# Gathering an expert's tokens: 32 one-hot products or an indirect DMA and 8 transposes

## What is computed

```python
def swiglu(h, w_gate, w_up, w_down):
    return (jax.nn.silu(h @ w_gate) * (h @ w_up)) @ w_down

def moe_ffn(h, w_router, w_gate, w_up, w_down):
    ...
    logits = (hf @ w_router).astype(jnp.float32)
    top_vals, top_idx = lax.top_k(logits, TOP_K)
    top_w = jax.nn.softmax(top_vals, axis=-1)
    gates = jnp.einsum('nk,nke->ne', top_w, jax.nn.one_hot(top_idx, N_EXPERTS, dtype=jnp.float32))
    out = jnp.zeros_like(hf)
    for e in range(N_EXPERTS):
        out = out + gates[:, e:e + 1].astype(hf.dtype) * swiglu(hf, w_gate[e], w_up[e], w_down[e])
```

## Time and profile before

| what | us |
|---|---|
| median of three runs | 1322.89 (1321.39 to 1323.42) |
| the profiled execution, its own time | 1321.78 |
| its span in the profile | 1320.0 |
| from the first gather's start to the last gather's last part | 504.5 to 1302.7 |

### The profile page before, as it was taken

One profiled execution on the slowest core, in us unless ns is written; L12 is line 12 of the kernel. 1 busy time (PEld: TensorE's weight loads), 2 busy tenths in 40 slices (PEclk: granted clock), 3 DMA queues, 4 the chain that ended last, 5 costly groups with the idle time before them and its releaser, 6 DMA issues.

```text
span 1320.0 us, 18637 instructions
## 1 busy us (share of the span) xinstructions
PE 1260.0 (95%) x6834; PEld 1070.5 (81%) x6834; DVE 1011.0 (77%) x1083; ACT 828.8 (63%) x877; POOL 117.7 (9%) x121
## 2 busy tenths in 40 slices
PE   6898899999899888999999999999999999999997
PEld 6776799999787676888888888888888888888885
DVE  5886654455579747888888888888888887887985
ACT  5356444433544745777777777777777777777774
POOL 2860000000069001000000000000000000000000
PEclk9899999999899797999999999999999999999998
DMA  9400665555442039999999999999999999999950
GB/s 327 147 20 1 206 215 190 182 179 184 123 156 76 17 120 361 377 361 327 356 366 328 351 364 332 347 367 329 348 365 329 350 364 329 348 363 332 349 216 32
DMA packets 174725, 344.40 MB, mean 261 GB/s; under 512 B 5558, under 2 KB 63476, under 8 KB 174676
## 3 DMA queue, kind: packets, MB, share of 16 engines
q1 hardware_dynamic: 173852, 341.27, 73.4%
q0 software_dynamic: 624, 1.93, 0.4%
q10 hardware_dynamic: 200, 0.54, 0.1%
HBM read 342.67 MB, written 1.05 MB: 260 GB/s over the span
## 4 chain that ended last, share of the span: by engine, by line
PE 87%; DVE 7%; ACT 3%; issue 2%; DMA 0%; SPq 0%; POOL 0%; POOLq 0%; DVEq 0%; ACTq 0%
PE bank L1432 26%; PE bank L1434 26%; PE bank L1433 26%; PE bank L1714 3%; PE bank L1734 1%; DVE cv L1086 1%; PE bank L1529 1%; DVE lo_ring L965 1%; DVE xn L1086 1%; ACT hi_ring L658 1%; PE bank L1569 1%; PE bank L1726 1%; PE bank L1727 1%; PE bank L1511 0%; DMA vec_rows<-in_diff_subln 0%
## 5 line engine op out<-in xcount | busy, mean ns | idle before, releaser
L970 DVE TENSOR_TENSOR lo_ring<-raw_m,hi_ring 128x2048 fp32r<-128x2048 f32 x168 | 382.6, 2288 | 51.2 <-ACT hi_ring L664 51.1
L664 ACT ACTIVATE hi_ring<-raw_m 128x2048 fp32r<-128x2048 f32 x168 | 322.2, 1919 | 84.6 <-PE bank L1434 84.6
L1432 PE MATMUL bank<-hi_ring,hT_hi 128*128 128x512 f32 (+2 forms) x896 | 336.3, 375 | 0.0
L1434 PE MATMUL bank<-hi_ring,hT_lo 128*128 128x512 f32 (+2 forms) x896 | 329.6, 368 | 0.0
L1433 PE MATMUL bank<-lo_ring,hT_hi 128*128 128x512 f32 (+2 forms) x896 | 329.0, 367 | 0.0
L970 DVE TENSOR_TENSOR lo_ring<-raw_a,hi_ring 128x2048 fp32r<-128x2048 f32 x96 | 219.3, 2291 | 41.0 <-ACT hi_ring L664 41.0
L664 ACT ACTIVATE hi_ring<-raw_a 128x2048 fp32r<-128x2048 f32 x96 | 183.4, 1918 | 57.5 <-PE bank L1434 57.5
L965 DVE TENSOR_TENSOR lo_ring<-raw_a,hi_ring 128x2048 fp32r<-128x2048 f32 (+2 forms) x59 | 131.8, 2236 | 96.3 <-ACT hi_ring L658 96.3
L1432 PEld LDWEIGHTS bank<-hi_ring,hT_hi 128*128 128x128 f32 x896 | 169.6, 189 | 30.6 <-DVE lo_ring L970 2.4
L1434 PEld LDWEIGHTS bank<-hi_ring,hT_lo 128*128 128x128 f32 x896 | 169.4, 189 | 28.7
L1433 PEld LDWEIGHTS bank<-lo_ring,hT_hi 128*128 128x128 f32 x896 | 169.7, 189 | 27.4 <-issue 0.5
(11 more groups left out here) (266 smaller groups left out, 1421.9 us busy)
## 6 DMA issues: line engine op xcount, KB each, us to landing
raw_m<-in_w_down_exp SPq DMA_DIRECT2D x80, 1024.0 KB, 5.4
raw_a<-in_w_up_exp SPq DMA_DIRECT2D x48, 1024.0 KB, 5.7
raw_m<-in_w_gate_exp SPq DMA_DIRECT2D x48, 1024.0 KB, 5.6
raw_a<-in_w_gate_exp SPq DMA_DIRECT2D x40, 1024.0 KB, 5.7
raw_m<-in_w_up_exp SPq DMA_DIRECT2D x40, 1024.0 KB, 5.9
raw_a<-in_w_in SPq DMA_DIRECT2D x12, 1024.0 KB, 7.0
raw_a<-in_w_gate_dense SPq DMA_DIRECT2D x11, 1024.0 KB, 5.4
raw_a<-in_w_up_dense SPq DMA_DIRECT2D x11, 1024.0 KB, 5.5
```

The lines of the kernel that those rows point to most:

```text
L664: A(hi_of(NA + j), t, ACT.Copy).then_inc(hi_ready, 1)
L970: V.tensor_tensor(lo_of(NA + j), expert_slot(i, j)[0], hi_of(NA + j).bitcast(F32), ALU.subtract).then_inc(lo_ready, 1)
L1432: M(o, lh, rh, start=start, stop=False)
L1434: return M(o, ll, rh, start=False, stop=stop)
```

## The change

- A new DRAM tensor `rows_dram` holds the normed rows with their gain, float32. POOL writes it from `xn` with two DMAs of 512 KB after line 627, ahead of its load of `g_bc`. ACT waits for both before its first step of item 0, since `m_sg` overwrites `xn`.
- Item 0 is gathered as before. For each later item PE makes two products of `onehot` with a column of token numbers, `tok_r`, after the first part of G4 of the item ahead; they give the token number of each slot. DVE casts it to an integer, `slot_i`, at the first part of U4. POOL then issues one indirect DMA: 128 rows of 4 KB from `rows_dram` into `xg`, which is the second half of `xn`.
- In the place of the 32 products stand 8 transposes of `xg`, into banks 6 and 7. ACT copies their high part into `sel_hi`, two instructions in the place of four; DVE subtracts it from the banks into `sel_lo`, two new instructions, ahead of `y_lo`. G0 of the next item now waits for DVE there.
- DVE no longer waits for the earlier gather before it makes a new `onehot`. ACT copies `tok_r` once in the setup, and the table of constants is 4 columns wider.

```diff
+            for t in range(TT):
+                pool.dma_start(rows_dram[t * P:(t + 1) * P, :], xn[:, t, :]).then_inc(rows_out, 16)
             pool.dma_start(g_bc[:], a["final_norm"].rearrange("(o d) -> o d", o=1).broadcast_to([P, D])
                            ).then_inc(gfin_in, 16)
+
+            def fetch(i, first=False):
+                if not first:
+                    pool.wait_ge(pad_done, i)
+                pool.wait_ge(slot_ready, i + 1)
+                nc.gpsimd.tensor_tensor(pool_pad[:], half_neg[:], half_neg[:], ALU.mult).then_inc(pad_done, 1)
+                nc.gpsimd.indirect_dma_start(xg, None, rows_dram, bass.IndirectOffsetOnAxis(slot_i[:, 0:1], 0),
+                                             bounds_check=T - 1, oob_is_err=False
+                                             ).then_inc(xg_in, 16)
+
+            pool.wait_ge(rows_out, 16 * TT)
+            fetch(0, first=True)
...
+            with pool.Fori(1, n_items) as i:
+                fetch(i)
             norm_pow(2 * LAYERS)
...
+            def fetched_evac(i):
+                for h in range(2):
+                    act.wait_ge(gather_mm, 4 + 2 * i + h + 1)
+                    A(sel_hi[:, 4 * h:4 * h + 4, :], bank[6 + h][:].rearrange("p (k s) -> p k s", k=4),
+                      ACT.Copy).then_inc(gathered, 1)
...
-                gather_evac(i + 1)
+                fetched_evac(i)
                 act.wait_ge(piece_used, expert_done(i, "D", EC - 1))
...
-            gather_evac(0)
+            first_gather_evac()
+            act.wait_ge(rows_out, 16 * TT)
             item(0, True)
...
-                        dve.wait_ge(gather_mm, 4 + 4 * i)
                         dve.wait_ge(onehot_done, 3 + 3 * i)
                         make_onehot(i + 1)
                         dve.wait_ge(route_v, rv[0] + 1 + i)
+                    if kind == "U" and c == 4 and part == 0:
+                        dve.wait_ge(slot_mm, i + 1)
+                        V.tensor_copy(slot_i[:], bank[7][:, 0:1]).then_inc(slot_ready, 1)
+                for h in range(2):
+                    dve.wait_ge(gathered, 4 + 2 * i + h + 1)
+                    V.tensor_tensor(sel_lo[:, 4 * h:4 * h + 4, :], bank[6 + h][:].rearrange("p (k s) -> p k s", k=4),
+                                    sel_hi[:, 4 * h:4 * h + 4, :].bitcast(F32), ALU.subtract).then_inc(gathered_lo, 1)
...
+            def slots_of(i):
+                pe.wait_ge(onehot_done, 6 + 3 * i)
+                for t in range(TT):
+                    r = M(bank[7][:, 0:2], onehot[:, t, :], tok_r[:, t, :], start=t == 0, stop=t == TT - 1)
+                r.then_inc(slot_mm, 1)
+
+            def fetched_transposes(i):
+                pe.wait_ge(xg_in, 16 * (i + 1))
+                for h in range(2):
+                    for kk in range(4):
+                        k = 4 * h + kk
+                        r = nc.tensor.transpose(bank[6 + h][:, kk * P:(kk + 1) * P], xg[:, k * P:(k + 1) * P], ident)
+                    r.then_inc(gather_mm, 1)
...
-                            gather(i + 1)
+                            fetched_transposes(i)
...
-                                pe.wait_ge(gathered, 3 + k // 4 + 4 * i)
+                                if first:
+                                    pe.wait_ge(gathered, 3 + k // 4)
+                                else:
+                                    pe.wait_ge(gathered_lo, k // 4 - 1 + 2 * i)
...
+                    if kind == "G" and c == 4 and part == 0:
+                        slots_of(i)
```

More of the change, by code:

```diff
@@ L162 @@
 K_BLK = K_R + QD
-K_END1 = K_BLK + P
+K_TOK = K_BLK + P
+K_END1 = K_TOK + 2 * TT
 K_MASK = 0
@@ L183, in tables @@
         one[h * DV:(h + 1) * DV, K_BLK + h * DV:K_BLK + (h + 1) * DV] = 1.0
+    for t in range(TT):
+        one[:, K_TOK + 2 * t:K_TOK + 2 * t + 2] = (t * P + np.arange(P))[:, None]
     two = np.zeros((P, K_END2), np.float32)
@@ L232, in build @@
         wr_parts = sb("wr_parts", [P, KT, 2, NE], F32R)
+        tok_r = sb("tok_r", [P, TT, 2], F32R)
+        rows_dram = nc.dram_tensor("rows_dram", (T, D), F32, kind="Internal").ap()
         mixers = ExitStack()
@@ L290, in build @@
         onehot_t = sb("onehot_t", [P, TT, P], F32R)
+        slot_i = sb("slot_i", [P, 1], U32)
+        pool_pad = sb("pool_pad", [P, 1])
         g_bc = sb("g_bc", [P, D])
@@ L335, in build @@
         m_sg, m_prod = spare[:, 0:EW], spare[:, EW:2 * EW]
+        xg = spare[:, 2 * EW:2 * EW + D]
         o_sq, o_rs, o_y, tap = (spare[:, 6 * P + m * T:6 * P + (m + 1) * T] for m in range(4))
@@ L422, in build @@
         ht_lo_done = sem("ht_lo_done")
+        rows_out = sem("rows_out")
+        slot_mm = sem("slot_mm")
+        slot_ready = sem("slot_ready")
+        xg_in = sem("xg_in")
+        pad_done = sem("pad_done")
+        gathered_lo = sem("gathered_lo")
         block = ctx.enter_context(nc.Block())
@@ L628, in _ @@
             pool.wait_ge(h_rows, 2)
+            for t in range(TT):
+                pool.dma_start(rows_dram[t * P:(t + 1) * P, :], xn[:, t, :]).then_inc(rows_out, 16)
             pool.dma_start(g_bc[:], a["final_norm"].rearrange("(o d) -> o d", o=1).broadcast_to([P, D])
                            ).then_inc(gfin_in, 16)
+            def fetch(i, first=False):
[8 more added lines that the diff above has]
+            fetch(0, first=True)
+            pool.wait_ge(items_ready, 1)
+            n_items = pool.value_load(it_i[0:1, 0:1], min_val=NE, max_val=ITEMS_MAX)
+            with pool.Fori(1, n_items) as i:
+                fetch(i)
             norm_pow(2 * LAYERS)
@@ L783, in _ @@
                         A(upper_r[:], upper, ACT.Copy)
+                        A(tok_r[:].rearrange("p t n -> p (t n)"), consts[:, K_TOK:K_TOK + 2 * TT], ACT.Copy)
                         A(ones_r[:], ones[:], ACT.Copy)
@@ L908, in _, with first_gather_evac @@
             A(e2[:], gap[:], ACT.Exp).then_inc(route_a, 1)
-            def gather_evac(i):
+            def first_gather_evac():
                 for h in range(4):
-                    act.wait_ge(gather_mm, 4 * i + h + 1)
+                    act.wait_ge(gather_mm, h + 1)
                     part, b = (sel_hi, bank[6 + h]) if h < 2 else (sel_lo, bank[h - 2])
@@ L1703, in _, with first_gather @@
             M(bank[5][:, 2 * NE:3 * NE], ones_r[:], chosen[:, 1, :], start=False, stop=True).then_inc(route_mm, 1)
-            def gather(i, first=False):
-                pe.wait_ge(onehot_done, 3 + 3 * i)
+            def first_gather():
+                pe.wait_ge(onehot_done, 3)
                 for src, b0, parts_done in ((ht_hi, 6, ht_split), (ht_lo, 0, ht_lo_done)):
-                    if first:
-                        pe.wait_ge(parts_done, TT)
+                    pe.wait_ge(parts_done, TT)
                     for h in range(2):
@@ L1778, in item @@
                         r.then_inc(onehot_tmm, 1)
-            gather(0, first=True)
+            first_gather()
             item(0, first=True)
```

## The result

The changed kernel takes 1314.6 us (1313.38 to 1315.41) beside 1321.55 us (1321.3 to 1323.42) for the kernel before: a ratio of 0.9944 with a 95% interval of 0.9931 to 0.9956, 7.0 us less. Forecast was 1315.6, counted from the 1322.89 us of an earlier measurement of the kernel before. A second measurement on another occasion gave 1313.63 us and 0.9945 (0.9928 to 0.9961).

The account below looks back on a forecast made before the run. PE was taken to bound the kernel. Seven item ends at 0.95 - 0.22 = 0.73 us give 5.1, the last item 2.2, together 7.3 off the earlier median: 1315.6 us, range 1309.0 to 1321.5.

Parts of the forecast that it names:

- The bound: Expert layer: PE bounds, busy throughout a 100 us stretch; its saved work is won unless something else was only just in time.
- D5: Products at an item's end that need `m_lo`: start 1.7 us earlier, not 2.5; 1.9 us after the `m_prod` transposes as sign.
- G0: Next item's first products: wait for DVE's `sel_lo`, start 0.95 us earlier (bounds 0.65 to 1.7), some 0.7 after D5's end.
- The slots: Two new PE products that find the token numbers: 0.22 us an item, at most 0.62.
- The sum: Seven item ends at 0.73 us each, 5.1, plus 2.2 for the last item: 7.3 us faster.
- The fetch: Indirect DMA into `xg`: costs nothing, 17.9 us from cast to need, 7.3 by the `g_bc` load, 10 to spare.
- rival 3: The fetch lands late, at 907.7, so D5 starts 2.0 us later than before; 18 us slower, 1341; 4%.
- The rows to DRAM: Two writes ahead of item 0: land between 507.3 and 514.6, in time for ACT's first split, nothing lost.
- Rival 1: Items' ends: `m_lo` and `sel_lo` come in time and all PE time saved is won, 18.3 us, 1304.6; 5%.
- Rivals 2 and 3: The first: ACT stands before item 0 for late row writes, 15.4 us lost, 1331.0, 5%; the second: see rival 3.
- Rival 4: The granted clock falls in PE's new gaps around D5, 3.4 us lost an item, 20 slower, 1343; 3%.
- Rival 5: DMA engines become the bound, with 350 GB/s as ceiling: an item takes 100.4 us, the kernel 1327.4; 2%.

Follow-up runs that it names:

- fill6: The changed kernel with 6 useless transposes added between the 8 transposes of fetched rows and D5: 1315.99 us, ratio to before 0.9952.
- early_m: The changed kernel with the last chunk's `m_prod` transposes, `m_hi` and `m_lo` moved between the two parts of D4, ahead of that step's split: 1313.46 us, ratio 0.994.
- slots10: The changed kernel with the two slot products made five times, ten in all: 1323.42 us, ratio to the kernel before 1.0014.
- latefetch: The changed kernel with slot products after G5 and the cast at U5, one chunk later: 1362.3 us, measured once.
- early_both: `early_m` with the fetched rows' transposes moved there too, and `sel_hi` and `sel_lo` ahead of the split at D5's step: 1303.52 us, ratio 0.9862.

## Why the prediction came out right

**The bound.** PE, with DVE just beneath it at one place. Right: the gain an item is not the 2.5 us by which PE has less to do.

**D5.** Forecast 1.7 us earlier with DVE's `m_lo` as what ends the wait; measured 1.71, and the wait 0.77 by the profile. The 1.09 taken for the transposes was 0.2 too much and did not matter, since `m_lo` came later. D5 starts 2.03 us after the transposes of `m_prod`, which is what the prediction's own 903.07 and 905.1 give; the 1.9 among its signs was counted from the gather. `fill6` shows that it is a wait, and `early_m` that it is fed by DVE's order.

**G0.** Forecast 0.95 us earlier, 0.7 us after D5's end; measured 1.00, and 0.66.

**The slots.** Taken at 0.22 from the gather's own products; `slots10` gives 0.22 for two. In their place in the item they cost 0.24: 0.15 to the product behind them and 0.09 by which that one's successor comes late. The upper bound of 0.62, from a product's duration from start to end, was far off: such products overlap.

**The sum.** Forecast 0.73 an item, measured 99.45 - 98.79 = 0.66. G0's 1.00 less 0.24 for the slots would be 0.76. The other 0.10 is not placed: beside the profile before, the changed kernel falls behind in steps of about 0.01 us spread over an item's products. Seven times 0.66 is 4.6, for a forecast 5.1. In the last item D5 comes 1304.63 - 1300.89 = 3.74 us after the start of the `m_prod` transposes before, and 1296.12 - 1294.81 = 1.31 now: 2.43 for a forecast 2.4, 2.2 with the slots. Together 6.8 us by the profile's items and 7.0 by the medians, for a forecast 7.3. The forecast of the time itself, 1315.6, is 1.0 too high mostly because the median that it was counted from, 1322.89, came out as 1321.55 in the comparison.

**The fetch.** Costed at nothing, with 10 us to spare by `g_bc`'s 7.3. It issues and lands in about that, 7.0 us, but the issue begins 2.4 us after the cast for the small product that DVE holds up, which the prediction did not count: in its rival 3 only casts and one-hot instructions could hold the fetch, and the splits did. Landing is at about 891.2 and the rows are wanted at 899.8: 8.6 us to spare. `latefetch` shows what the cover is worth.

**The rows to DRAM.** Forecast to land between 7.3 and 14.6 us after issue and to cost nothing. The DMA issues of the changed kernel (count, KB each, median us to landing; the second line is the fetch):

```profile
rows_dram<-xn POOLq DMA_DIRECT2D x2, 512.0 KB, 8.2
...
xn<-rows_dram,slot_i POOLq DMA_INDIRECT x8, 7.0
```

They took 8.2 us, and ACT's first split of item 0 starts right behind its last copy, with no wait:

```profile
510.37 1.90 ACT L696 ACTIVATE hi_ring<-raw_a 128x2048 fp32r<-128x2048 f32 x1
```

**The rivals.** Rival 1, that all is won, is what the kernel could have done and did not; `early_both` is 17.8 us under the kernel before by its own pair of medians. Rivals 2 and 3 came about only with four times the writes, and with the fetch a chunk later. Rival 4: the clock did not fall for waits of 0.77 and 0.49 us, and fell in `latefetch` for 6.5. One of the stretches that the prediction sets beside this rival says less than was read from it. From 494 to 500 the clock stayed at 1.00, but from 502.4 on it stood at 0.50 for 13.6 us, after PE had been busy for 0.16 of the 2.3 us from 500; the kernel before:

```profile
502.40:516.00 13.60, 12.33 (x48) 11.28 (x48) 11.17 (x57) 4.19 (x5) 0.00 (x0) 0.50 1.04 398
```

Rival 5: the DMA engines moved 357 GB/s in the changed kernel and 364 in `early_both`, and no engine waited for a load in the expert layer of either; the ceiling is above that. The figure of 358 GB/s a core that the Trainium skill gives (HBM Reference, "Specifications (TRN2)") is no ceiling for this core here: the kernel with 364 shows it, and the page says as much for a core that streams alone.

## What to carry to other kernels

Before work is taken off the bounding engine, look what other engines do during it: what they finish just in time is the new bound, and there may be two such in a row. Here taking away the first wait alone won 0.27 us an item, and taking away both 1.65. Small instructions of DVE stood behind splits of 2.3 us that nobody needed yet; put ahead of them, with the transposes and copies that feed them, they turned a gain of 7 us into one of 18. What a wait is worth can be tested by filling it with useless work.

## What was not expected of the hardware

- A POOL product of 128x1 took 2.16 us when a DVE `tensor_tensor` with both inputs in SBUF started 0.17 us before it, and 0.18 us when DVE stood still. An indirect DMA's instruction took 1.02 us on POOL when it started behind such a split and 0.3 us ahead of the next, and 2.81 us when it started 0.38 us into one. The Trainium skill (SBUF — State Buffer, "Who interferes with whom") says that a DVE instruction with two SBUF inputs contends with a GpSimd instruction that reads SBUF; these rows agree. For the instruction of the fetch, what it reads there was not told apart.
- G0's first product after a wait takes 0.34 us to the next one's start (806.40 to 806.74) where without a wait it takes 0.23, so that this wait costs 0.11 us beyond the gap before it. D5's first product does not show this: 0.33 us behind the wait (802.85 to 803.18), but 0.32 behind transposes without one (895.67 to 895.99 in `early_both`) and 0.29 behind the gather (906.81 to 907.10, before).
- The small product with DVE still, a multiplication, takes 0.18 us, and POOL's `pow` products of the same shape 0.56 us. They differ in the operation and in their inputs; which of the two counts was not told apart.
